# Second block's mixers: four engines' orders laid out anew with a fourth place for high parts of weights, and the state cleared early

## What is computed

```python
proj = h @ w_in                       # 7096 columns: fox, mla, dn (delta rule), gates
# fox: causal attention with a decay, 8 heads of 64
y_fox = fox_out @ w_br_fox
# mla: q and k/v come through small "latents"; parts of q and k are rotated by position
q  = (rmsnorm(mla_cq,  g) @ mla_w_uq)     # 768 columns
kv = (rmsnorm(mla_ckv, g) @ mla_w_ukv)    # 1024 columns
k_full = concat(k_nope, rotate(k_rope)); q_full = concat(q_nope, rotate(q_rope))
y_mla = causal_attention(q_full, k_full, v) @ w_br_mla
# dn: short convolution and silu on q, k, v; then a chunked delta rule with a state per head:
#   (I + M)^-1 of 64x64 blocks by doubling (2, 4, 8, 16, 32), and a scan over chunks of the state
y_dn = (rmsnorm(o) * silu(z)) @ w_br_dn
return (g_fox * y_fox + g_mla * y_mla + g_dn * y_dn) @ w_out
```

## Time and profile before

| | us |
|---|---|
| median of 3 runs | 2070.62 (2069.84 to 2071.89) |
| the profiled execution | 2069.9 |
| its span in the profile | 2068.1 |
| PE busy in it | 2015.6 (97%) |
| DVE, ACT, POOL busy in it | 1289.6, 878.0, 193.2 |

### The profile page before, as it was taken

How to read it: one execution, slowest core, us unless ns; L and a number is a source line. 1 busy time by engine, 2 the same in 40 slices (tenths; PEclk the granted TensorE clock), 3 DMA queues, 4 the chain that set the end, 5 groups by cost and what they waited for, 6 DMA issues and landing times.

```text
span 2068.1 us, 36059 instructions
## 1 busy us (share of the span) xinstructions
PE 2015.6 (97%) x15397; PEld 1813.4 (88%) x15397; DVE 1289.6 (62%) x1716; ACT 878.0 (42%) x1264; POOL 193.2 (9%) x218
## 2 busy tenths in 40 slices
PE   6999999999999999899999999999998999999998
PEld 6999989999878889799988888888897999888887
DVE  4675364674467778753536777776778545357775
ACT  4544134443154446553422444444465543324443
POOL 0300013000100001400101000000014011110000
PEclk9999999999999999999999999999999999999999
DMA  6455445555456665333324666566654333235663
GB/s 219 161 168 163 163 153 173 164 164 163 160 156 189 196 185 161 110 103 103 112 79 138 184 186 194 170 184 190 198 160 131 103 106 111 92 122 163 189 198 133
DMA packets 347734, 320.38 MB, mean 155 GB/s; under 512 B 9931, under 2 KB 317752, under 8 KB 347576
## 3 DMA queue, kind: packets, MB, share of 16 engines
q1 hardware_dynamic: 345800, 317.60, 48.5%
q10 hardware_dynamic: 1776, 0.48, 0.1%
HBM read 317.01 MB, written 1.05 MB: 154 GB/s over the span
## 4 chain that ended last, share of the span: by engine, by line
PE 93%; DVE 2%; ACT 2%; DMA 1%; issue 1%; POOL 1%; SPq 0%; DVEq 0%; POOLq 0%; ACTq 0%
PE banks L1120 17%; PE banks L1121 16%; PE banks L1122 16%; PE banks L1184 16%; PE banks L1115 9%; PE banks L1183 7%; PE banks L1590 3%; PE banks L1141 3%; PE banks L1186 1%; ACT ring_high L1728 1%; DVE ring_low L2036 1%; PE banks L1321 1%; PE banks L1308 1%; DMA ring<-in_w_in 1%; PE banks L1656 0%
## 5 line engine op out<-in xcount | busy, mean ns | idle before, releaser
L2036 DVE TENSOR_TENSOR ring_low<-ring,ring_high 128x2048 fp32r<-128x2048 f32 x272 | 628.0, 2310 | 345.7 <-ACT ring_high L1728 344.1
L1728 ACT ACTIVATE ring_high<-ring 128x2048 fp32r<-128x2048 f32 x272 | 519.5, 1911 | 226.2 <-PE banks L1122 143.0
L1184 PE MATMUL banks<-hT_low,ring_high 128*128 128x512 f32 x1376 | 475.0, 396 | 0.0
L1120 PE MATMUL banks<-hT_low,ring_high 128*128 128x256 f32 x1344 | 390.8, 291 | 0.0
L1121 PE MATMUL banks<-hT_low,ring_high 128*128 128x256 f32 x1344 | 380.3, 283 | 0.0
L1122 PE MATMUL banks<-hT_low,ring_low 128*128 128x256 f32 x1344 | 380.1, 283 | 0.0
L1183 PE MATMUL banks<-hT_low,ring_low 128*128 128x256 f32 x1204 | 335.8, 279 | 0.0
L1184 PEld LDWEIGHTS banks<-hT_low,ring_high 128*128 128x128 f32 x1376 | 248.3, 188 | 47.9
L1728 ACT ACTIVATE scratch<-banks 128x256 f32<-128x256 f32 (+3 forms) x302 | 130.4, 449 | 315.8 <-PE banks L1141 126.8
L1120 PEld LDWEIGHTS banks<-hT_low,ring_high 128*128 128x128 f32 x1344 | 257.7, 192 | 5.2 <-issue 2.6
L1121 PEld LDWEIGHTS banks<-hT_low,ring_high 128*128 128x128 f32 x1344 | 257.8, 192 | 0.6 <-issue 0.5
(11 more groups left out here) (201 smaller groups left out, 2483.4 us busy)
## 6 DMA issues: line engine op xcount, KB each, us to landing
ring<-in_w_in SPq DMA_DIRECT2D x122, 1024.0 KB, 5.0
ring<-in_ffn_w_gu SPq DMA_DIRECT2D x176, 512.0 KB, 4.7
ring<-in_ffn_w_down SPq DMA_DIRECT2D x44, 1024.0 KB, 4.9
ring<-in_w_out SPq DMA_DIRECT2D x16, 1024.0 KB, 4.9
ring<-in_w_branch SPq DMA_DIRECT2D x12, 1024.0 KB, 4.9
ring<-in_w_br_mla SPq DMA_DIRECT2D x4, 1024.0 KB, 4.9
ring<-in_w_br_fox SPq DMA_DIRECT2D x4, 1024.0 KB, 4.9
ring<-in_w_br_dn SPq DMA_DIRECT2D x4, 1024.0 KB, 4.9
```

The costliest lines, as they stand in the source:

```text
L1120: pe.matmul(acc, lhs[0], rhs[0], start=start, stop=False)
L1184: mm = pe.matmul(acc[:, :], lhs(k)[0], h_pair[:, :, k], start=(k == 0), stop=(k == KD - 1))
L1728: return act.activation(o, i, ACT.Copy)
L2036: return dve.tensor_tensor(o, i0, i1, op)
```

## The change

`HIGHS` goes from 3 to 4: a fourth place of 2048 columns for high parts. In exchange `scratch` shrinks from 23480 to 22160 columns: one half of `mv` moves to `gates_` (so `d(26)`, which writes there, waits on ACT for the last mla values), `m_junk` lies on a part of `mqk`, and 24 columns of the small tiles' room go. The strings of all four engines are written anew. `DENSE_ORDER` has piece 23 after pieces 2 to 7. DVE clears `d_S` in `small_values2`, at the mixer's beginning, and no longer at `X1.0.0`. Where it matters below: on PE `dh.15` and `d.15` stand before the `u.0.1` products and `dh.16` before `L1.0.0`; `MT.1.0` stands after `Y.0.2.0`; `X1.0.0` stands before `U.0.1` and `R1.1.0`. On DVE `d.14` and `d.15` stand before `DP2`; the splits of pieces 17, 18 and 19 stand between `K1.0.0` and `Z.0.2.0`, and that of 16 right before `QK.0.0`. On ACT no split stands any more between `u.1.0` and `u.1.1`. Outside the mixers, the fourth piece's split of the first block's layers and of the first feed-forward parts comes one step earlier.

```diff
-HIGHS = 3
+HIGHS = 4
@@
-DENSE_ORDER = [0, 1, 8, 9, 10, 11, 12, 13, 14, 15, 16, 17, 18, 19, 20, 21, 22, 23, 2, 3, 4, 5, 6, 7, 24, 25, 26, 27]
+DENSE_ORDER = [0, 1, 8, 9, 10, 11, 12, 13, 14, 15, 16, 17, 18, 19, 20, 21, 22, 2, 3, 4, 5, 6, 7, 23, 24, 25, 26, 27]
 MIX = {
     "PE": (
-        "FFFFFFMFFFFFMQQFUFFFQQFQUUDUUUDDUUDDTAATAAFDAADAADAFDAFDAFDAFDAAFDAFDAAFDAFDAAFDAFDDAADADFDAAD"
-        "FDADFDAADAAFDAADFDAFDAFDFDFDFDFDDXDDFDXFDXFDXXDFDADFDFDADFDAFDAFDAAFDADFDDADADFDADFAAFDADFDAAFDA"
-        "DFDAADADFDAADAADADAFDXAFXFXFXXFFX"
+        "FFFFFFMFMFFFFQQFFUFQQFQFDFUUUUUDDUUDDAATTFDAADAADAADADFDAFDAFDAFDAFDAADFDDADFDAAFDADFFDAAFD"
+        "ADFDAADAFDAADFDAADAADFDAFDAXDDDDFXDFXDFXXDFDFDAFDAFDAFDADFDAAFDAFDAADADFDDAAFDDADFDAAFDADFDAADAD"
+        "FDAADAADADAFDAFDFDFXDFXFXFXXFFX"
     ),
     "ACT": (
-        "FWFWMMFWFCWFCFCWQQCWFUCFQQWCFUQUWDUUUDDUUWTAATAADAADAAAFDWAAFDWAAAFDWAAAFDWAAAFDWADAADDDAFAAWDDA"
+        "FFMWFMWFCWWFCFCFQQCWWFCUQQCFQWFUDUUUUDDUUWWTATAWDAADAAAADAFDAAWFDAAAWFDAAADWFDADDDAAWFWAFDAADWAF"
...
     "DVE": (
-        "WMWMCWCCWCCMCCWMWCCCNQNDNNCCDWDWDWFDAAFWDAWDAWDAWDAWDAADDDWADWDADWADWDWDXWDXDDXWXXXDXWADADWDAWDA"
+        "MMWCWMCMWWCCCCCCWWCCNQFNDFNNWDCCDWDWWDADADWADWADWADDWADDWAADWDAWDDAWDADXXDWXDDXXXWXDAWADWADWDADA"
...
     "POOL": (
-        "MNNUUKDDDDDKDDDDDKDDXDDDKDDDDDFFXFF"
+        "MNNUUKDDDDDKDDDDDKDXDDDDKDDDDDFFXFF"
     ),
 }
@@
-        SCRATCH = 23480
+        SCRATCH = 22160
...
-        mv = r.take(t=TT, n=512)
+        mv_0 = r.take(n=512)
...
+        mv = mv_0, g.take(n=512)
...
-        m_junk = g.take(t=TT, n=M_QR + M_KVR)
+        m_junk = v(mqk[:, 0].rearrange("p t n -> p (t n)")[:, 0:TT * (M_QR + M_KVR)], t=TT, n=M_QR + M_KVR)
@@ def d2 (ACT)
-                    if o == 16:
+                    if o == 26:
+                        act.wait_ge(*filled(L, ("V", "mla", 7)))
+                    elif o == 16:
                         act.wait_ge(*m_roped(L, 2))
@@ def small_values2 (DVE)
             def small_values2(L):
+                dve.memset(d_S, 0.0).then_inc(state_zero.sem, 1)
                 dve.wait_ge(*zlog_done(L, 1))
@@ def d_x1 (DVE)
                 if (t, c) == (0, 0):
-                    dve.memset(d_S, 0.0).then_inc(state_zero.sem, 1)
                     dve.wait_ge(*state_zero(L, 1))
```

More of the change, by code:

```diff
@@ L244, in takes @@
     return s[0] in TAKES[engine]
-DENSE_ORDER = [0, 1, 8, 9, 10, 11, 12, 13, 14, 15, 16, 17, 18, 19, 20, 21, 22, 23, 2, 3, 4, 5, 6, 7, 24, 25, 26, 27]
+DENSE_ORDER = [0, 1, 8, 9, 10, 11, 12, 13, 14, 15, 16, 17, 18, 19, 20, 21, 22, 2, 3, 4, 5, 6, 7, 23, 24, 25, 26, 27]
 MIX = {
     "PE": (
-        "FFFFFFMFFFFFMQQFUFFFQQFQUUDUUUDDUUDDTAATAAFDAADAADAFDAFDAFDAFDAAFDAFDAAFDAFDAAFDAFDDAADADFDAAD"
-        "FDADFDAADAAFDAADFDAFDAFDFDFDFDFDDXDDFDXFDXFDXXDFDADFDFDADFDAFDAFDAAFDADFDDADADFDADFAAFDADFDAAFDA"
-        "DFDAADADFDAADAADADAFDXAFXFXFXXFFX"
+        "FFFFFFFMFMFFFFQQFFUFQQFQFDFUUUUUDDUUDDAATTFDAADAADAADADFDAFDAFDAFDAAFDAFDAADFDDADFDAAFDADFFDAAFD"
+        "ADFDAADAFDAADFDAADAADFDAFDAXDDDDFXDFXDFXXDFDFDAFDAFDAFDADFDAAFDAFDAADADFDDAAFDDADFDAAFDADFDAADAD"
+        "FDAADAADADAFDAFDFDFXDFXFXFXXFFX"
     ),
     "ACT": (
-        "FWFWMMFWFCWFCFCWQQCWFUCFQQWCFUQUWDUUUDDUUWTAATAADAADAAAFDWAAFDWAAAFDWAAAFDWAAAFDWADAADDDAFAAWDDA"
-        "FAAWDAAAADFWADFWDFWDFDWDDDFWDDFWDAFDWADAFWADAAFWDADADDDAFAAAFDDAAAFDADAADAAADAAADADAXX"
+        "FFMWFMWFCWWFCFCFQQCWWFCUQQCFQWFUDUUUUDDUUWWTATAWDAADAAAADAFDAAWFDAAAWFDAAADWFDADDDAAWFWAFDAADWAF"
+        "DAAWDAAADAAFAADWAFDDDDDWFWDFDWAFDAAWFDAWDAAFADAAWDAFDADADDAFAADDAFAADADAAAADAAFDADDXX"
     ),
     "DVE": (
-        "WMWMCWCCWCCMCCWMWCCCNQNDNNCCDWDWDWFDAAFWDAWDAWDAWDAWDAADDDWADWDADWADWDWDXWDXDDXWXXXDXWADADWDAWDA"
-        "WDDADDADAADFDAFDDAFXFXFXFXXFXF"
+        "MMWCWMCMWWCCCCCCWWCCNQFNDFNNWDCCDWDWWDADADWADWADWADDWADDWAADWDAWDDAWDADXXDWXDDXXXWXDAWADWADWDADA"
+        "WDADDDAADADDADFDFFXFXFXFXXFXF"
     ),
     "POOL": (
-        "MNNUUKDDDDDKDDDDDKDDXDDDKDDDDDFFXFF"
+        "MNNUUKDDDDDKDDDDDKDXDDDDKDDDDDFFXFF"
     ),
@@ L647, in build @@
         small = Room(scratch, SCRATCH, r.at)
-        r.at += 640
+        r.at += 616
         conv_from = r.at
@@ L669, in build @@
         d_cross = r.take(n=512)
+        both_at = r.at
         both = r.take(w=2, h=8, n=SEQ)
         mqkT = both
-        fox = Room(scratch, r.at, r.at - 4096)
-        mv = r.take(t=TT, n=512)
+        fox = Room(scratch, r.at, both_at)
+        mv_0 = r.take(n=512)
         fqT = fox.take(j=4, n=SEQ)
@@ L677, in build @@
         neg_c = fox.take(n=SEQ)
-        dn_T = v(scratch[:, r.at - 5120:r.at - 4096], j=4, n=SEQ)
+        dn_T = v(scratch[:, both_at:both_at + 4 * SEQ], j=4, n=SEQ)
         br_tmp2 = v(at_sc[:, :, :, :].rearrange("p u c n -> p (u c n)"), u=2, n=512)
@@ L691, in build @@
         cT3 = g.take(j=3, n=SEQ)
-        early = Room(scratch, r.at, r.at - 5120)
+        early = Room(scratch, r.at, both_at)
         craw = early.take(u=2, j=2, n=SEQ)
@@ L1352, in values @@
                 else:
-                    vals = fv if kind == "fox" else mv
+                    vals = (fv[:, 0], fv[:, 1]) if kind == "fox" else mv
                     for c in range(2):
@@ L1357, in values @@
                                     lambda kb: at_wT[:, u % 2, (c * nk + kb) * P:(c * nk + kb + 1) * P],
-                                    lambda kb: vals[:, kb, h * HD:(h + 1) * HD], nk)
+                                    lambda kb: vals[kb][:, h * HD:(h + 1) * HD], nk)
                 mm.then_inc(fills(L, ("V", kind, u)), 1)
@@ L1938, in up @@
                     copy(v(mqk[:, 1, t], h=8, n=M_QK)[:, hs, 0:HD], src[:, :, 0:HD])
-                    copy(v(mv[:, t], h=8, n=HD)[:, hs, :], src[:, :, HD:P]).then_inc(drains(L, step), 1)
+                    copy(v(mv[t], h=8, n=HD)[:, hs, :], src[:, :, HD:P]).then_inc(drains(L, step), 1)
             def mla_turned(L, t, w, h_):
```

## The result

The changed kernel takes 2080.53 us (median of 5 runs, 2078.27 to 2084.89) where the kernel before took 2069.84 on the same chip: 10.7 us more, ratio 1.0051, interval 1.0041 to 1.0062. The forecast was 2069.6 with a range up to 2074.5. It was wrong, and on the other side.

A forecast was written before the change was run, and what follows sets the result against it. PE, busy for 97% of the span, bounds the kernel; only its waits, about 15 us, can be won. Mixers of 311.2 us each give - 1.7 and + 0.7, together - 1.0: 2069.6 us, range 2063.5 to 2074.5.

The forecast's parts named there:

- Outside the second block's mixers nearly nothing changes: Rest of the kernel: no change counted, except up to 0.3 us in one layer for the fourth piece's earlier split.
- the rivals: Three other outcomes: rotations not held longer (2063.4 to 2065.6, chance 0.36), DVE late (2077.6, 0.12), clearing without gain (2072.6 to 2074).
- The slower rival: DVE runs 2 us or more late at the end of stage I: + 8, 2077.6 us; chance 0.12.
- stage I: Mixer from d.0 to u.0.3: two halves come in, + 6.1, a gap goes, - 0.5; 58.59 becomes 64.2 us.
- Stage II: Mixer from u.0.3 to Y.0.2.0: POOL's chain ends last and sets its length, 20.2 us, bounds 18.2 to 22.3.
- POOL's chain: POOL's two rotations, KW.0.0 and the level for Y.0.2.0: 16.2 us with three DVE splits beside it, 18.2 with four.
- the fourth split: One more DVE split beside POOL's work before Y.0.2.0, where three stood: + 2.0 us.
- in two waits: PE idle about 7 us between u.0.3 and Y.0.2.0, at MT.0.0 and at Y.0.2.0, 4 to 6 before the latter.
- Stage III: Mixer from Y.0.2.0 to the dn branch: two halves leave, MT.1.0 comes in, X1.0.0's wait goes; 226.8 us in both layers.
- The clearing: State cleared early, so the wait before X1.0.0 goes: - 1.5 us per layer, - 1.5 more in the first for the clock.
- The fourth lead piece: Outside the mixers: the fourth piece's earlier split may hold DVE for up to 0.3 us in one layer.
- The Trainium skill's rule: DVE and POOL take shared SBUF ports in turn: a fourth split adds 2.3 to 2.7, stage II 20.5 to 20.9 us.

The follow-up runs named there:

- e1: The changed kernel with the turn of the ring slots put at piece 16 (gu 0 12) instead of piece 104 (down 9), orders kept: 2070.83 us.
- e4: e1 with DVE's splits of pieces 17 to 21 later, so one split instead of four stands beside POOL's chain: 2065.85 us.
- e5: e4 with DT.0.2, DT.1.2 and dh.16 ahead of MT.0.0 on PE and in ACT's readings: 2060.59 us.
- e3: The kernel before with only the clearing of the state moved to the mixer's beginning: 2065.89 us.
- e7: The changed kernel's memory, four high places and early clearing, under the orders of the kernel before: 2067.51 us.
- e9: e5 with the split of gu 0 3 put behind gu 0 0 again, as with three high places: 2060.06 us.
- e6: e3 with DVE's splits of pieces 16 and 17 later, so one split instead of three stands beside POOL's chain: 2062.20 us.

## Why the prediction was wrong

**"Outside the second block's mixers nearly nothing changes": this step failed.** It was written on the lists and on the places of the splits; the slots of the loads come from the same lists, through the plan, and weren't followed. In its place the runs show two loads that come 5.6 us late at the end of each layer, with a wait of 3.04 and 1.86 of lowered clock in the first: 9.7 us in two layers, and none of the rivals had it. The slower rival was put into stage I, where it didn't happen. None of the rows ahead of the prediction shows it, but the trace of before could have priced it. Down 10's load, issued at 1305.54, lands 5.7 later, just when ACT's split of it begins (1311.24), so nothing is spare there. DVE is through with the split and the two low parts behind it at 1316.16, and PE wants them at 1317.74: 1.6 of slack. A load that waits one piece longer comes 5.6 later: an estimate of 5.6 - 1.6 = 4.0 us of waiting. 3.04 came, since in the changed kernel that load took 5.1 and not 5.7, and one of the two low parts (0.34) is done ahead of the split.

**The mixers: right in size, off in one place.** Stage I was put at 64.2: it was 65.86 and 65.26, and 64.18 and 63.77 in e1, which has the same lists; what lies between is the clock at half in dh.15. Stage II was put at 20.2: 19.41. Its mechanism held (POOL's chain 17.45 with four splits beside it, 17 to 19.5 expected, and Y.0.2.0 follows its end at 878.95 by 0.10); the term that was too large is the fourth split, put at 2.0, with which the chain grew by 1.3. PE is idle for 6.3 us there, about 7 expected "in two waits", but they are divided otherwise: 4 to 6 us were expected before Y.0.2.0 and 0.80 stood. The large one is one link earlier:

```profile
864.22 0.46 PE L1582 MATMUL banks<-scratch 64*64 64x64 f32 x16 [0.79 <-DVEq L2440]
869.39 1.91 PE L1143 MATMUL banks<-const,gates 128*96 128x128 f32 x8 [4.71 <-POOL gates L2733]
```

K1.0.0 waits 0.79 (under 1 expected, 2.49 before), then MT.0.0 waits 4.71 for the first rotation, which two of the four splits hold. In the changed kernel the chain's end still decides the stage; once three splits are out of the chain (e4), the wait at MT.0.0 decides it, and covering that is worth 1.6 to 1.9 us per layer more (e5). Stage III was put at 226.8: 227.06 in both. Together 311.2 was forecast, 312.34 and 311.73 came. For both mixers - 1.0 was forecast against before; it was + 0.7 in the changed kernel's execution and - 2.5 in that of e1 (310.63 and 310.24), which has the same lists.

**The clearing** was counted at - 1.5 in each layer and - 1.5 more in the first for the clock: - 4.5. Alone it gave - 4.5 in the two stages III of e3 and - 3.8 in the median. So the new lists and the fourth place give back all of it: e1, which has all three, is at 2070.83, 4.9 above e3. Of that the mixers are 2.0 (310.63 + 310.24 less 309.93 + 308.94) and the fourth lead piece 1.0.

**The fourth lead piece** was put at up to 0.3 in one layer: it cost 1.0 to 1.1 (e7, e9). The place was right, the size off by three times: the wait isn't DVE's time for a split but that of a load not yet landed. It shows in the second layer of e1 as well (193.22), but not in that of the changed kernel (192.26), where the layer before has ended 4.9 us later and the load, it seems, has the time; no run tests that reason. The first layer's 0.2 stands in the changed kernel too and not in e9.

**The Trainium skill's rule** (SBUF — State Buffer, section "SBUF: two separate sides") says that such a DVE operation and a POOL operation that reads SBUF take the shared ports in turn, each for its whole instruction. The runs agree that each split stops a POOL operation, at 1.87 to 2.23 us; a POOL operation that began 0.04 us behind the split of piece 19 (876.12 and 876.08) lost 2.08 of that split's 2.29. The full 2.3 to 2.7 that the prediction worked out by the rule didn't come. Two of the splits became longer beside the chain (2.79 and 2.54, alone 2.29), which fits a split that waits for a running POOL operation; no run here separates that.

Of the 10.7 us, 9.7 are gone in e1, and the two ends of the profiled executions differ by the same 9.7. That the two agree is in part chance: e1 also took on the 1.0 of the lead piece's wait, and its mixers were 3.2 shorter in the profiled executions, by the clock in dh.15 alone. The remaining 1.0 is e1 against before, a sum of - 3.8 for the clearing and + 4.9 for the rest, of which 1.9 is not placed; the first block's two layers took 596.7 to 601.4 in ten profiled executions, with no order by kernel, so the traces can't place it.

## What to carry to other kernels

When an order is written anew, follow everything that is computed from it, not only what stands in it: here the ring's slots, and through them two loads 200 us behind the mixer's end, decided the result. A buffer's turn belongs where the loads have a whole piece to spare, and not in the last pieces ahead of a boundary. And where one engine's long operations stop another's short ones, move them past the end of the waited-for chain, then see which link PE waits for next (e4, then e5): the two together gave 10 us. The second alone wasn't tried; in the changed kernel it could have won little, since POOL's chain ends last there.

## What the runs showed of the hardware

- A wait of PE can cost more than itself: 3.04 of waiting came with about 1.9 of lowered clock in the first layer (4.9 in all), and e5, which has no wait above 1.3 in stage II, kept the granted clock at 1.00 there, where after's was 0.82. It isn't always so: e6 waited 2.1 in the first layer's stage II at 1.00, and e9, with e5's waits, had half the clock for 3.41 us in the second layer's.
- DVE's split and POOL's operations slow each other: the three taken away gave POOL 6.2 us, and two of them had themselves been 0.25 and 0.50 longer beside it (2.54 and 2.79 for 2.29).
- The clock also falls without any wait: in dh.15, right behind DG's twenty small products, in both layers of the changed kernel (4.56 for 3.07), in the first layer of e4, and in neither layer of e1 or e5, with the same steps. What decides it stayed open.
